# The gated-delta recurrence of a hybrid trunk layer: products of the inverse ahead of those of its transpose, in banks of their own, and another order around them

## The chip, the cores and the metric

The kernel runs on one core of a Trainium2 chip. The metric is the device time of one execution in microseconds. Three runs of the kernel before took 4781.29, 4789.78 and 4797.11 us; the median is 4789.78 us.

## The reference

One layer of a diffusion trunk is computed for 128 context tokens and 512 latent tokens, all in fp32: an adaLN-modulated RMSNorm, one input projection, two token mixers (a bidirectional chunked gated DeltaNet with 8 heads of 128, and a chunked spatial-gating MLP), branch and output projections, and a retrieval of experts (16384 single-neuron experts, 8 heads, top 16). What matters here is the DeltaNet:

```
S_t = exp(g_t) (I - beta_t k_t k_t^T) S_{t-1} + beta_t k_t v_t^T ;  o_t = S_t^T q_t / sqrt(dk)

decay = exp(where(causal, gc_i - gc_j, -inf))          # gc: cumulative log decay in a chunk
m   = where(strict, (beta k) k^T * decay, 0);  tri = m + I
u, w = tri^-1 [beta v, beta k exp(gc)]
qk  = q k^T * decay
per chunk:  v_new = u - w S
            o = (q exp(gc)) S + qk v_new
            S = S exp(g_last) + (k exp(g_last - gc))^T v_new
```

It runs forward and backward in time, for the context from a zero state, for the latent tokens from a given state.

## The kernel before, in words

The kernel takes chunks of 128 tokens, one a batch. The function `deltanet` runs once for the context (one block of tokens, two directions: two batches) and once for the latent tokens (four blocks, two directions: eight batches, n = 0 to 7). All eight heads of a batch are worked together. Five engines have instruction streams written out by hand, in a fixed order, tied by semaphores.

The inverse of `tri` is built by doubling. `x_` holds the inverse, `xt` its transpose, both 128 x 8 x 128, in two copies that alternate by batch. `begin` sets level 0 from the matrix m (`m_`) and its transpose (`mt`). For each level k = 1 to 6:

- POOL multiplies `mt` by the mask of the level (`masked`, L927) into one of two buffers `lev`;
- PE multiplies `lev` by `x_` (L992 or L999) into banks 4 and 5: the sub-products, in two halves u of four heads;
- ACT copies each half to `pm` (L1215);
- PE multiplies on the left by `xt` and on the right by `xt` (`changed_products`, L1010), giving what changes in `x_` (not at level 6) and in `xt`. Before, both results of a half lie side by side in bank 2 + u, and each half is released by one semaphore, `q_ps`;
- DVE adds them into `x_` and `xt`, four additions of 128x256 (L1142, L1144).

Around the levels, a batch also turns k and v by the identity (L987, into banks 6 and 7, and 0 and 1), multiplies them by gates on DVE (`kbe`, `kd`, `vn`), and prepares the next batch n + 1: PE makes the decay sums (`decays`, banks 0 and 1) and the gram matrix (banks 6 and 7) after level 4 and the q k scores (`scores_of`, banks 0 and 1) after level 5; DVE makes the `differences` for masking after level 4 (L1105, sixteen operations) and the `strict` product after level 5 (L1117, eight). In `finish` PE makes w (half_products into banks 4 and 5), turns m of the next batch (`turn_m`), and makes v_new (L1057, L1058), o (L1066, L1067) and the new state's addend. DVE then runs `begin` for the next batch (L1125 to L1134), takes o (L1178 or L1180, banks 4 and 5) and adds the state (L1185), which releases `batch_done`. PE's turning of k for the next batch waits for `batch_done`; so does POOL's `state` (L948: the state times its decay; then L951: queries times their decay). At the fifth latent batch (n = 4) the state is loaded anew for the other direction, after `batch_done`.

Beside this, 28 gathered rows of experts for the context tokens are used in the latent recurrence, four in each of the batches 0 to 6: POOL issues an indirect gather of 1 MB (`gather_until`, L350) into one of three slots, once the row that had the slot has been used, and DVE takes a dot product per row (`use_rows`, L396). Before, rows 0 to 3 of a batch are used ahead of level 1, after the additions of level 4, after the strict product of level 5, and between the two halves of o (in batch 0 the first at level 3). POOL issues the gathers after mask 3, after mask 6, and two after the first two masks of the next batch.

## Time and profile before

| | us |
|---|---|
| profiled execution, span from first to last instruction | 4786.7 |
| timed runs, median of 3 (4781.29 to 4797.11) | 4789.78 |
| latent recurrence, 1198.36 to 1569.04 of the span | 370.7 |
| steady latent batch (1248.03 to 1292.99) | 44.96 |

The span is that of one profiled execution; what lies around the span in that execution is not recorded separately, so the span stands beside the timed runs. In the rows below, times are microseconds from the start of the span. PE is TensorE, PEld its weight loads, DVE is VectorE, ACT is ScalarE, POOL is GpSimd. A timeline row gives the start, the duration, the engine, the line of the kernel, the operation, what it writes and reads, how many instructions are merged, and in brackets how long the engine was idle before it and whom it waited for.

### The profile page before, as it was taken

The numbers are of one execution on the slowest core, as the hardware profiler recorded it, in microseconds if no ns is written. First come the engines' busy times: TensorE is split into PE (matmuls) and PEld (weight loads), VectorE is DVE, ScalarE is ACT, GpSimd is POOL, SyncE is SP. The second block draws the span as 40 slices with busy tenths as digits, with TensorE's granted clock in tenths as the row PEclk, the third lists the DMA queues.
The fourth block names the chain that finished last, engine by engine and source line by source line (L and its number), as shares of the span: only waits on it lengthen the run. The fifth ranks groups of instructions, "written<-read, shape, count | busy, mean of one in ns | idle before, by whom it ended". The sixth has DMA issues, their size and how long they took to land.

```text
span 4786.7 us, 61495 instructions
## 1 busy us (share of the span) xinstructions
PE 4559.0 (95%) x25813; PEld 3365.2 (70%) x25813; DVE 3043.3 (64%) x4399; ACT 579.6 (12%) x1080; POOL 1656.3 (35%) x1110
## 2 busy tenths in 40 slices
PE   6989999999888999899999998999999999999997
PEld 2776346444888544347555545699999999999997
DVE  1451006888877777417777667988865557886556
ACT  1531001441222100000000001110000000000000
POOL 0131001674655554210544443433432332322221
PEclk8999999999999999999999999999999999999998
DMA  9919898997322998997999997579999999999998
GB/s 400 383 63 368 314 347 321 384 393 288 110 83 90 361 390 352 421 369 270 408 420 420 411 413 300 220 294 420 418 417 421 405 406 419 417 417 419 404 420 326
DMA packets 237328, 1663.47 MB, mean 348 GB/s; under 512 B 28231, under 2 KB 32729, under 8 KB 37787
## 3 DMA queue, kind: packets, MB, share of 16 engines
q0 software_dynamic: 130048, 939.72, 48.6%
q1 hardware_dynamic: 98884, 673.84, 35.6%
q10 hardware_dynamic: 8120, 45.98, 2.4%
q8 instruction: 204, 3.34, 0.3%
q14 instruction: 72, 0.58, 0.0%
HBM read 1639.68 MB, written 18.94 MB: 347 GB/s over the span
## 4 chain that ended last, share of the span: by engine, by line
PE 43%; DVE 6%; DMA 5%; issue 1%; POOL 1%; ACT 0%; ACTq 0%; DVEq 0%; POOLq 0%
PE ps L242 25%; PE ps L2415 14%; DMA arena_sb<-peer_v,arena_sb 4%; DVE arena_sb L401 2%; PE ps L2357 1%; PE ps L1815 1%; DMA arena_sb<-peer_u,arena_sb 1%; POOL arena_sb L350 1%; DMA x_rows<-arena_sb 0%; DVE arena_sb L2117 0%; DVE arena_sb L2107 0%; DVE arena_sb L2109 0%; DVE arena_sb L2190 0%; DMA arena_sb<-w_query 0%; DVE arena_sb L2114 0%
## 5 line engine op out<-in xcount | busy, mean ns | idle before, releaser
L242 PE MATMUL ps<-arena_sb 128*128 128x224 f32 (+3 forms) x9728 | 2292.2, 396 | 10.7 <-PEq L579 6.2
L242 PEld LDWEIGHTS ps<-arena_sb 128*128 128x128 f32 x9728 | 1669.6, 191 | 627.2 <-issue 335.0
L401 DVE SCALAR_TENSOR_TENSOR arena_sb<-arena_sb 128x2048 f32<-128x2048 f32 x412 | 988.7, 2400 | 460.8 <-DMA arena_sb<-peer_v,arena_sb 431.3
L396 DVE CUSTOM_DVE_ANT_0 arena_sb<-arena_sb 128x2048 f32<-128x2048 f32 x416 | 977.7, 2366 | 306.5 <-DMA arena_sb<-peer_u,arena_sb 305.8
L350 POOL DMA_INDIRECT arena_sb<-peer_v,arena_sb x416 | 617.6, 1485 | 1147.9 <-DVE arena_sb L401 918.4
L350 POOL DMA_INDIRECT arena_sb<-peer_u,arena_sb x416 | 642.2, 1544 | 811.2 <-DVE arena_sb L396 462.4
L2415 PE MATMUL ps<-arena_sb 128*128 128x224 f32 x4096 | 776.3, 352 | 1.3 <-ACT arena_sb L2454 0.6
L2415 PEld LDWEIGHTS ps<-arena_sb 128*128 128x128 f32 x4096 | 774.4, 190 | 1.9 <-issue 1.0
L1625 PE MATMUL ps<-arena_sb 128*128 128x512 f32 x768 | 342.8, 603 | 25.3 <-DMA arena_sb<-w_gb_r 10.2
L1625 PEld LDWEIGHTS ps<-arena_sb 128*128 128x128 f32 x768 | 145.6, 193 | 217.7 <-issue 197.0
L1815 PE MATMUL ps<-arena_sb 128*128 128x512 f32 x640 | 277.7, 596 | 4.4 <-DMA arena_sb<-w_out 2.2
L288 POOL DMA_DIRECT2D arena_sb<-w_mod x64 | 34.8, 544 | 590.8 <-PE ps L249 478.0
L1815 PEld LDWEIGHTS ps<-arena_sb 128*128 128x128 f32 x640 | 121.8, 191 | 159.5 <-issue 153.6
L927 POOL TENSOR_TENSOR arena_sb<-arena_sb 128x1024 f32<-128x1024 f32 x60 | 159.8, 2682 | 185.6 <-ACT arena_sb L1206 175.6
L1682 DVE TENSOR_TENSOR arena_sb<-ps,arena_sb 128x512 f32<-128x512 f32 x16 | 11.1, 692 | 288.9 <-PE ps L1625 288.9
L249 PE MATMUL ps<-arena_sb,scond_sb 128*32 128x512 f32 x768 | 128.4, 703 | 33.0 <-DMA arena_sb<-w_mod 33.0
L1340 PE MATMUL ps<-arena_sb 128*128 128x512 f32 x320 | 138.4, 593 | 0.8 <-DMA arena_sb<-w_vg 0.4
L1010 PE MATMUL ps<-arena_sb 128*64 128x32 f32 (+1 forms) x3520 | 122.9, 228 | 5.0 <-ACT arena_sb L1215 2.5
L1010 PEld LDWEIGHTS ps<-arena_sb 128*64 128x64 f32 x3520 | 114.0, 143 | 11.4 <-ACT arena_sb L1215 6.1
L2604 DVE TENSOR_SCALAR arena_sb<-arena_sb 128x128 f32<-128x128 f32 x448 | 119.7, 353 | 0.0
L1340 PEld LDWEIGHTS ps<-arena_sb 128*128 128x128 f32 x320 | 60.5, 190 | 78.1 <-issue 75.8
L2454 ACT ACTIVATE arena_sb<-ps 128x224 f32<-128x224 f32 (+27 forms) x107 | 28.9, 270 | 676.9 <-PE ps L242 676.9
(288 smaller groups left out, 2983.7 us busy)
## 6 DMA issues: line engine op xcount, KB each, us to landing
arena_sb<-peer_ut SPq DMA_DIRECT2D x128, 1024.0 KB, 9.3
arena_sb<-peer_vt SPq DMA_DIRECT2D x128, 1024.0 KB, 9.2
arena_sb<-w_mod POOLq DMA_DIRECT2D x64, 1024.0 KB, 9.2
arena_sb<-w_qkv SPq DMA_DIRECT2D x48, 1024.0 KB, 9.2
arena_sb<-w_out SPq DMA_DIRECT2D x48, 1024.0 KB, 7.4
arena_sb<-w_query SPq DMA_DIRECT2D x48, 1024.0 KB, 6.9
arena_sb<-w_mod SPq DMA_DIRECT2D x32, 1024.0 KB, 8.8
arena_sb<-w_ga_r SPq DMA_DIRECT2D x32, 1024.0 KB, 7.8
```

The costliest lines, as they stand in the source:

```text
L242: mm = pe.matmul(out, weights[:, k * P:(k + 1) * P], x[:, k, :], start=(k == 0), stop=(k == chunks - 1))
L249: mm = pe.matmul(out[32 * j:32 * j + 32, :], t.scond[:, k + j, :], weights[:, j * COL:(j + 1) * COL], start=start, stop=stop, tile_positio ...
L350: nc.gpsimd.indirect_dma_start(slot, None, a["peer_v" if adds else "peer_u"], bass.IndirectOffsetOnAxis(ap=seg.index[:, p:p + 1], axis=0)) ...
L396: nc.vector.tensor_tensor_reduce(rows, rows, total, 1.0, 0.0, ALU.mult, ALU.add, seg.dots[:, p:p + 1]).then_inc(t.rows_used, 1)
L401: nc.vector.scalar_tensor_tensor(out=total, in0=rows, scalar=seg.weight[:, p:p + 1], in1=total, op0=ALU.mult, op1=ALU.add).then_inc(t.rows ...
L927: nc.gpsimd.tensor_tensor(lev[:, k % 2], mt, over(nmask[:, 1 - r, k], H), ALU.mult).then_inc(s["level_masked"], 1)
L1010: mm = pe.matmul(compact(bank(2 + u), k, side)[rows, h % 4, a], lhs[:, h, rows], changed(rhs, k, second)[:, h, a], start=True, stop=True, ...
L1340: mm = pe.matmul(t.ps[:, 4 * c + b, :], h[:, k, b * P:(b + 1) * P], tile_slot(t, H + 4 * c + kq)[:, kk * COL:(kk + 1) * COL], start=(k == ...
L1625: mm = pe.matmul(t.ps[:, s, :], x[:, k, :], tile_slot(t, n)[:, kk * COL:(kk + 1) * COL], start=(k == 0), stop=(k == 4 * tiles - 1))
L1815: mm = pe.matmul(t.ps[:, 4 * (c % 2) + b, :], merged[:, k, b * P:(b + 1) * P], tile_slot(t, 4 * c + kq)[:, kk * COL:(kk + 1) * COL], start ...
L2415: mm = pe.matmul(t.ps[:, bank_of[h][first + i], 0:DENSE], ring[slot_of[n - 1]][:, col:col + P], acts[:, s, :], start=(s == 0 and h == 0), ...
L2604: nc.vector.tensor_scalar(weighted[i][:, u], t.pick_iota, key1[:, e:e + 1], weight[:, e:e + 1], ALU.is_equal, ALU.mult)
```

## The change

- The left products (what changes in `x_`) go to bank 2 for all eight heads, the right products (what changes in `xt`) to bank 3. All left products of a level are issued before the right ones, and each side has one semaphore (`left_ps`, `right_ps`) per level.
- DVE adds each side in one operation of 128x512 and releases `x_done` after the left one and `xt_done` after the right one. The sub-products of level k + 1 wait for `x_done` alone and are issued right behind the right products of level k.
- A batch starts with the sub-products of level 1; the turning of v and then of k follow them. Each half of those sub-products waits until DVE has read that half of the last o (`o_read`), since it overwrites its bank.
- For the next batch: decays are issued after the sub-products of level 4, the gram matrix after those of level 5, the scores after the last right products, ahead of w. `differences` is split: a half after level 4, a half after level 5; the strict product comes after level 6. ACT's exponents are split likewise.
- DVE makes `vn` at level 1, `kbe` at level 2 and `kd` at level 3.
- POOL makes mask 3 right behind the state's scaling, then two gathers, the staging of the next gates, masks 4 to 6, the queries' product, and a gather; after the first two masks of the next batch, one more.
- The 28 rows stay four a batch. Rows 0 to 3 are used ahead of level 1, at level 3, after `begin`, and between the halves of o. In batch 0, rows 0 and 1 are used after level 6, ahead of `begin`.

```diff
-            for u in range(2):
-                pe.wait_ge(s["x_done"], 13 * n + 1 + (2 * (k - 2) + u + 1 if k > 1 else 0))
-                products_of(4, u, lev[:, k % 2], x_[n % 2]).then_inc(s["p_ps"], 1)
-            for u in range(2):
-                pe.wait_ge(s["p_copied"], 12 * n + 2 * (k - 1) + u + 1)
-                if k < LEVELS - 1:
-                    changed_products(1, u, xt[n % 2], pm, k, r)
-                changed_products(0, u, pm, xt[n % 2], k, 1 - r).then_inc(s["q_ps"], 1)
+        def sub_products(n, k, u):
+            pe.wait_ge(s["level_masked"], 6 * n + k)
+            pe.wait_ge(s["x_done"], 6 * n + k)
+            if k == 1:
+                after(pe, s["o_read"], 2 * (n - 1) + u + 1)
+            products_of = paired_products if 1 < k < LEVELS - 1 else half_products
+            products_of(4, u, lev[:, k % 2], x_[n % 2]).then_inc(s["p_ps"], 1)
+        def left_products(n, r, k):
+            after(pe, s["xt_done"], 6 * n + k - 1)
+            for u in range(2):
+                pe.wait_ge(s["p_copied"], 12 * n + 2 * (k - 1) + u + 1)
+                mm = changed_products(2, u, xt[n % 2], pm, k, r)
+            mm.then_inc(s["left_ps"], 1)
+        def levels(n, r, j, b):
+            for u in range(2):
+                sub_products(n, 1, u)
+            pe.wait_ge(s["tok_done"], n + 1)
+            turned(0, tokens(heads[:, 16:24], b)).then_inc(s["vtok_ps"], 1)
+            after(pe, s["batch_done"], n)
+            pe.wait_ge(s["mt_copied"], 2 * n + 2)
+            turned(6, tokens(heads[:, 8:16], b)).then_inc(s["ktok_ps"], 1)
+            for k in range(1, LEVELS):
+                if k < LEVELS - 1:
+                    left_products(n, r, k)
+                right_products(n, r, k)
+                if k < LEVELS - 1:
+                    for u in range(2):
+                        sub_products(n, k + 1, u)
+                if n + 1 < 2 * nb:
+                    if k == 3:
+                        decays(n + 1, *order[n + 1])
+                    if k == 4:
+                        gram(n + 1, *order[n + 1])
         def finish(n, r, j, b):
+            if n + 1 < 2 * nb:
+                scores_of(n + 1, *order[n + 1])
...
@@ DVE
         def level(n, r, k):
+            if k < LEVELS - 1:
+                dve.wait_ge(s["left_ps"], 5 * n + k)
+                dve.wait_ge(s["x_done"], 6 * n + k)
+                cols = changed(x_[n % 2], k, r)
+                nc.vector.tensor_tensor(cols, cols, compact(2, k), ALU.add).then_inc(s["x_done"], 1)
+            dve.wait_ge(s["right_ps"], 6 * n + k)
+            after(dve, s["xt_done"], 6 * n + k - 1)
+            cols = changed(xt[n % 2], k, 1 - r)
+            nc.vector.tensor_tensor(cols, cols, compact(3, k), ALU.add).then_inc(s["xt_done"], 1)
...
+                elif k == 3:
+                    nc.vector.tensor_tensor(kd, banks(6), wide(tail, P), ALU.mult).then_inc(s["ktok_read"], 1)
+                    if n:
+                        use_rows(dve, nc, t, rows[1:2])
+                elif n + 1 < 2 * nb:
+                    if k == 6:
+                        strict(n + 1, *order[n + 1])
+                    else:
+                        differences(n + 1, k - 4, *order[n + 1])
+            if n == 0:
+                use_rows(dve, nc, t, rows[0:2])
             if n + 1 < 2 * nb:
                 begin(n + 1, *order[n + 1])
+            use_rows(dve, nc, t, rows[2:3])
...
@@ POOL
+            scale_state(n, *at)
+            masked(n, r, 3)
+            if 0 < n < loads:
+                gather_until(pool, nc, t, a, min(behind[n].start + 3, t.rows))
             if n + 1 < 2 * nb:
                 stage(n + 1, *order[n + 1])
+            for k in range(4, LEVELS):
+                masked(n, r, k)
+            scale_queries(n, *at)
+            if n == 0 and loads:
+                pool.wait_ge(h_out, 16)
+                gather_until(pool, nc, t, a, behind[0].start + 3)
+            elif n < loads:
+                gather_until(pool, nc, t, a, min(behind[n].start + 4, t.rows))
             if n + 1 < 2 * nb:
                 first_levels(n + 1, *order[n + 1])
             if n < loads:
+                gather_until(pool, nc, t, a, min(behind[n].start + 5, t.rows))
```

SP's loads of the next stage wait for `right_ps` at the point where they waited for `q_ps`. In the output projection the list of rows gets another length for groups whose entries are all zero.

## Rows read from the trace of the kernel before

**Rows 1.** The page, its part 1: busy time of the engines.

```profile
PE 4559.0 (95%) x25813; PEld 3365.2 (70%) x25813; DVE 3043.3 (64%) x4399; ACT 579.6 (12%) x1080; POOL 1656.3 (35%) x1110
```

**Rows 2.** Windows, one a latent batch: stretch, us, busy us, clock, DMA share, GB/s.

```profile
1198.36:1248.03 49.67, 42.32 (x672) 40.30 (x672) 41.73 (x67) 14.07 (x24) 29.29 (x16) 0.92 0.31 108
...
1248.03:1292.99 44.96, 39.53 (x680) 37.55 (x680) 38.59 (x67) 13.74 (x24) 28.73 (x14) 1.00 0.27 96
...
1337.95:1383.62 45.67, 41.33 (x680) 39.26 (x680) 38.39 (x67) 13.85 (x24) 28.77 (x14) 0.96 0.27 94
...
1383.62:1440.92 57.30, 45.27 (x680) 43.44 (x680) 38.38 (x67) 13.84 (x24) 27.03 (x14) 0.82 0.25 84
...
1532.30:1569.04 36.74, 35.39 (x620) 32.97 (x621) 14.36 (x29) 10.84 (x17) 13.69 (x6) 0.95 0.47 191
```

**Rows 3.** Timeline of PE in the steady batch (n = 1).

```profile
1248.09 1.09 PE L987 MATMUL ps<-ident_sb,arena_sb 128*128 128x128 f32 x8 [2.02 <-DVE arena_sb L1185]
...
1250.89 2.09 PE L1010 MATMUL ps<-arena_sb 128*64 128x64 f32 x64
...
1257.82 1.15 PE L999 MATMUL ps<-arena_sb 128*64 128x64 f32 x32 [1.40 <-POOL arena_sb L927]
...
1259.20 2.06 PE L1010 MATMUL ps<-arena_sb 128*64 128x32 f32 x64 [0.23 <-ACT arena_sb L1215]
...
1272.35 2.05 PE L982 MATMUL ps<-arena_sb 128*128 128x128 f32 x16 [0.42 <-DVE stat_sb L1109]
...
1276.12 1.44 PE L1010 MATMUL ps<-arena_sb 128*64 128x64 f32 x32
...
1278.29 2.05 PE L992 MATMUL ps<-arena_sb 128*128 128x128 f32 x16 [0.72 <-DVE arena_sb L1144]
```

**Rows 4.** Timeline of DVE at the end of that batch.

```profile
1273.55 2.15 DVE L1117 SCALAR_TENSOR_TENSOR arena_sb<-ps,beta_sb,arena_sb 128x128 f32<-128x128 f32 x8
...
1282.37 1.23 DVE L1132 TENSOR_TENSOR arena_sb<-arena_sb 128x1024 f32<-128x1024 f32 x1 [0.40 <-ACT arena_sb L1206]
...
1283.62 3.26 DVE L1134 TENSOR_TENSOR arena_sb<-arena_sb,ident_sb 128x1024 f32<-128x1024 f32 x1
...
1287.41 3.84 DVE L396 CUSTOM_DVE_ANT_0 arena_sb<-arena_sb 128x2048 f32<-128x2048 f32 x1
...
1291.17 0.68 DVE L1178 COPY arena_sb<-ps 128x512 f32<-128x512 f32 x1
...
1291.78 1.21 DVE L1185 TENSOR_TENSOR arena_sb<-arena_sb,ps 128x1024 f32<-128x1024 f32 x1
...
1292.90 2.28 DVE L396 CUSTOM_DVE_ANT_0 arena_sb<-arena_sb 128x2048 f32<-128x2048 f32 x1
```

**Rows 5.** Timeline of POOL over the same end and the next head.

```profile
1282.41 6.68 POOL L927 TENSOR_TENSOR arena_sb<-arena_sb 128x1024 f32<-128x1024 f32 x2 [13.07 <-ACT arena_sb L1206]
...
1289.25 2.85 POOL L350 DMA_INDIRECT arena_sb<-peer_u,arena_sb  x1 [0.15 <-issue]
...
1293.37 3.58 POOL L948 TENSOR_TENSOR arena_sb<-arena_sb 128x1024 f32<-128x1024 f32 x1
...
1297.04 2.39 POOL L951 TENSOR_TENSOR arena_sb<-arena_sb 128x1024 f32<-128x1024 f32 x1
...
1299.37 1.04 POOL L957 COPY gate_rows_sb<-g_sb 128x1024 f32<-128x1024 f32 x1
```

**Rows 6.** Timeline of POOL after the state's reload (n = 4).

```profile
1393.13 1.91 POOL L948 TENSOR_TENSOR arena_sb<-arena_sb 128x1024 f32<-128x1024 f32 x1 [9.15 <-issue]
```

**Rows 7.** Timeline of DVE at the head of the latent stage.

```profile
1191.57 3.37 DVE L1132 TENSOR_TENSOR arena_sb<-arena_sb 128x1024 f32<-128x1024 f32 x1
...
1194.97 3.24 DVE L1134 TENSOR_TENSOR arena_sb<-arena_sb,ident_sb 128x1024 f32<-128x1024 f32 x1
```

**Rows 8.** POOL's masks, L927: duration ns min/median/max, first and last start.

```profile
L927 POOL TENSOR_TENSOR arena_sb<-arena_sb x47: 2327/2367/3391, 1193.8 to 1547.9; 128x1024 f32<-128x1024 f32 x47
```

**Rows 9.** DMA issues of the latent stage: count and median us to landing.

```profile
arena_sb<-peer_u,arena_sb POOLq DMA_INDIRECT x28, 7.1
```

More of the change, by code:

```diff
@@ L960, in _ @@
         for n, at in enumerate(order):
[L961 removed]
+            r = at[0]
+            scale_state(n, *at)
+            masked(n, r, 3)
+            if 0 < n < loads:
+                gather_until(pool, nc, t, a, min(behind[n].start + 3, t.rows))
             if n + 1 < 2 * nb:
                 stage(n + 1, *order[n + 1])
[L964 to L970 removed]
+            for k in range(4, LEVELS):
[6 more added lines that the diff above has]
+                gather_until(pool, nc, t, a, min(behind[n].start + 4, t.rows))
             if n + 1 < 2 * nb:
@@ L973, in _ @@
             if n < loads:
-                gather_until(pool, nc, t, a, min(behind[n].start + 6, t.rows))
-            if n < loads:
-                gather_until(pool, nc, t, a, min(behind[n].start + 7, t.rows))
+                gather_until(pool, nc, t, a, min(behind[n].start + 5, t.rows))
     @block.tensor
@@ L1071, in _ @@
         decays(0, *order[0])
+        gram(0, *order[0])
         scores_of(0, *order[0])
@@ L1074, in _ @@
         for n, at in enumerate(order):
-            r, j, b = at
-            pe.wait_ge(s["tok_done"], n + 1)
-            turned(0, tokens(heads[:, 16:24], b)).then_inc(s["vtok_ps"], 1)
-            after(pe, s["batch_done"], n)
-            pe.wait_ge(s["mt_copied"], 2 * n + 2)
-            turned(6, tokens(heads[:, 8:16], b)).then_inc(s["ktok_ps"], 1)
-            for k in range(1, LEVELS):
-                level(n, r, k)
-                if n + 1 < 2 * nb:
-                    if k == 4:
-                        decays(n + 1, *order[n + 1])
-                    if k == 5:
-                        scores_of(n + 1, *order[n + 1])
+            levels(n, *at)
             finish(n, *at)
@@ L1177, in _ @@
                 if r == 0:
-                    nc.vector.tensor_copy(out, bank(4 + u))
+                    nc.vector.tensor_copy(out, bank(4 + u)).then_inc(s["o_read"], 1)
                 else:
-                    nc.vector.tensor_tensor(out, out, bank(4 + u), ALU.add)
-                if n < loads and u == 0:
-                    use_rows(dve, nc, t, behind[n][3:4])
+                    nc.vector.tensor_tensor(out, out, bank(4 + u), ALU.add).then_inc(s["o_read"], 1)
+                if u == 0:
+                    use_rows(dve, nc, t, rows[3:4])
             dve.wait_ge(s["state_scaled"], n + 1)
@@ L1208, in _ @@
         root(0)
-        exponents(0)
+        for u in range(2):
+            exponents(0, u)
         transposed(0)
```

119 lines of the change are left out of this document (51 added, 68 removed).

## The prediction

> **What bounds the kernel now.** I read the page first: TensorE is busy 95% [rows 1] of a span of 4786.7 us. An average over such different stages prices nothing, so I cut the recurrence with the view of windows, one window per batch, each ending where DVE's state addition (L1185) ends. Write B for that end. The reader is to see latent batches of 45 to 57 us, the last of 37, and a granted clock between 0.82 and 1.00 in them [rows 2]; from 1198.36 to 1569.04 they take 370.7 us, or 7.7% of the span. DMA's share is 0.25 to 0.47 there, so no stream of weights hides a change of this stretch. Last come the timelines of one steady batch: B = 1248.03 to B = 1292.99, 44.96 us at clock 1.00.
>
> In it PE is busy for 39.5 us and waits at four places: 2.02 us for B before it turns k; 1.40 us for the third mask from POOL; 0.42 us before the scores; 0.72 us before w [rows 3]. At the end it is DVE that sets B. Write M for the moment when the turned matrix has been copied (L1132 starts, 1282.37). From M to B are 10.62 us [rows 4], while PE has its last o and s products out 7.6 us after M.
>
> **Inside a level nothing is gained.** A level takes 1.38 us from the first sub-product to the first corrected product (1257.82 to 1259.20), then 2.06 us of products: 3.44 us [rows 3]. After: the left products (1.03) first, the right ones (1.03) behind them. The wide addition to x starts when the left ones have drained (some 0.17 us) and takes about 0.68, the nearest row being the 128x512 copy L1178 [rows 4]; 0.85 us of it fit behind 1.03 us of right products, so the next sub-products follow at once: 1.38 + 2.08 = 3.46. DVE has fewer instructions, which is worth nothing while PE sets the pace. Own banks and separate semaphores cost nothing either.
>
> **Steady batch after, from B to M.** PE's times after B:
> - Head. Sub-products 1 now come before the two turnings and half of them wait for `o_read` of the second half, about 1.15 us before B. So u1 runs to B - 0.2, v is turned to 0.8, k to 1.7, level 1 ends at 3.8. Before: k turned and sub-products (1248.09 to 1250.89), then level 1 (2.09), ended at 4.95 [rows 3]. Gain 1.2.
> - Levels 2 and 3 end at 7.24 and 10.7. The third mask is there: POOL's state scaling ends at 3.96 because it is pushed behind DVE's row (3.58 us instead of 1.91 [rows 5, 6]), the mask adds 2.35 [rows 8]: 6.3. The old stall of 1.40 is gone.
> - What is late next is the fourth mask. Behind the third stand two gathers (0.95 + 0.30 each, 2.5), the staging (1.04) and its own 2.35: 12.3. With row 0 not yet landed DVE loses the first place on the port and all is some 0.15 later. PE is ready at 10.7 to 11.8, so it stalls to 12.45.
> - Sub-products 4 (1.12), decays (1.88) and products (2.08): 17.53. The additions behind the row that now stands at level 3 come 0.2 late: 17.74. Level 5 with the gram matrix in its gap: 22.82. Both gaps hide 0.26 us of copying each. Sub-products 6 (1.88) and the last right products (1276.12 to 1277.56, 1.44 [rows 3]): 26.14, against 29.54 before.
> - Then scores (1.88, which cover DVE's last addition, so the 0.72 of before is saved), w (1.88), turning and copying m: M at 32.1, against 34.34. **Gain to M: 2.25 us.** The difference halves, 2.07 us each, follow the additions of levels 4 and 5 and end before the scores want them.
>
> **From M to B.** Here the change gives it back. Before, DVE after L1132 does L1134 (3.26), a half of o, a row (3.84, though the next one takes 2.28), a half of o, the state [rows 4]. After, the row that stood behind the strict products (L1117) stands here as well: 0.6 + 2.2 us more of DVE in front of a B that DVE sets. The rows show what it meets: DVE operations with both inputs in SBUF and POOL's masks do not overlap. POOL's two masks run 1282.41 to 1289.09 (6.68, where 2 x 2.35 would be 4.7), one of them and L1134 wait for each other, the row waits for the second, and the gather behind them takes 2.85 instead of 0.95 [rows 4, 5]. So after: masks gone at M + 6.7, row 2 to M + 8.8, o (0.60), row 3 (2.21), o (0.60), state (1.20): B = M + 13.4. And DVE is late: last addition, strict products (2.15 [rows 4]) and three passes of begin, some 1.14 each, end at M + 0.5, so that POOL takes the port first, as at the head of the stage where L1132 took 3.37 and L1134 3.24 [rows 7]. Then B = M + 14.0. Against 10.62: **loss 2.8 to 3.4 us**. Batch: 32.1 + 13.9 = 46.0, or **+1.05** (bounds -1.6, were none of it to wait for POOL: M + 11.3; and +2.4, were row 0 of the next batch late by as much as its gather can be: landing takes a median of 7.1 us from issue [rows 9], and its issue lies at the end of the masks, so that it lands about 1 us after B).
>
> The Trainium skill (SBUF — State Buffer, section Who interferes with whom) says that a DVE instruction with two SBUF inputs and a GpSimd one that reads SBUF exclude each other, and that issue order decides who blocks. The rows agree (3.26 against 1.23, 3.58 against 1.91); the rule speaks against moving a row behind `begin`, where both masks run.
>
> **The other batches.**
> - n = 0: PE turns v and k (1.9) after sub-products 1 instead of before; rows 0 and 1 (4.4) lie ahead of begin, and row 3 is gathered only after the next masks, and waits for its landing. The stall that row 1 made in this batch goes. By the same walk B comes 2.7 to 7.3 later than in its 49.67 us; I take +5.
> - n = 1, 2, 3, 5, 6: 5 x 1.05 = +5.2.
> - n = 4, state reloaded: POOL's scaling starts 9.5 us after B [rows 6], the third mask is now next (13.8 instead of 17.1 after B), but the fourth stands behind gathers and staging at 19.7. 55.5 against 57.30: -1.8 (bounds -4 and 0).
> - n = 7, no rows: head -1.2, w now waits for the whole last addition, +0.9: -0.3.
> - Context: masks of n = 1 start 2.39 earlier (the query product, L951 [rows 5], is now behind them), -0.6 in n = 0, +0.9 for the last w: -2.0.
> - Clock. The batch at 0.96 took 0.7 us more than the one at 1.00 [rows 2]. Now the head has two idle pieces of about 2 us with 0.94 of work between, where it had one of 2.02; I take three more batches at the lower level: +2.1 (bounds 0 and 12).
>
> The Trainium skill (TensorE: Matmul & The Clock Gate, section HAM oscillation) has it that waits between short bursts return the array to half clock again and again. This trace shows it in part: 0.82 in the batch with the long wait, 1.00 in one with four short ones [rows 2].
>
> Sum: 5 + 5.2 - 1.8 - 0.3 - 2.0 + 2.1 = +8.2 us on the profiled span of 4786.7. What lies around that span is not shown; the median of the timed runs, 4789.8, is 3.1 above it. Prediction **4798 us**. Row count after the stage, `behind` in the output projection and the loads of w_z are as before: 0, since the list only changes its length for groups whose entries are all zero.
>
> **Rivals.**
> - *Faster.* The tail: if POOL's masks let DVE through, row 2 ends 2.2 after L1134 and not after the masks, B = M + 11.3. Place: DVE between M and B; price -2.7 per row batch. It decides wherever the tail falls under 12.9 us after M, which is 10.62 + 2.25. Then six batches give -1.6, n = 0 about +1, n = 4 -4, context and n = 7 -2.3: about -15, or 4775. For: L1132 at 1.23 was let through before the mask. Against: L1134 (3.26) and the row behind it (3.84) [rows 4].
> - *Nothing gained or lost.* Only the order of DVE and POOL at M falls the lucky way and row 0 lands in time: +0.3 a batch, n = 0 +2.7, the rest -4: 4790.
> - *Slower by clock.* The two idle pieces bring the lower level in all batches, twice in some: 12 in place of 2: 4808.
> - *Slower by landing.* Row 0, gathered behind two masks, row 2 and its own 0.95, lands 2 to 3 us after B; left addition 1 stands behind it on DVE, and PE behind that. The fourth mask's stall absorbs 1.7 of it: +1.4 x 6: 4806.
> - That it doesn't do what it says: with no difference beyond the moved row, +2.2 x 7: 4805, held in the two above.
>
> **Numbers.** Forecast 0.42, faster rival 0.13, nothing 0.18, clock 0.15, landing 0.12. The range takes in the second, fourth and fifth and most of the first: 4780 to 4812. A time 0.3% (14.4 us) off 4789.8 can be told from no change: under 4775.4 faster, over 4804.2 slower. Half of the faster rival lies under its bound, and a little of my own error: 0.12. The two slow rivals and the upper end of the forecast: 0.27. Same: 0.61.
>
> **What would show it.** Steady batches of 46 us; third-mask stall gone, one of about 1.7 us before sub-products 4; no wait before w; M 2.2 us earlier after B; 13.4 to 14.0 us from M to B with two rows in it, the first stretched by POOL; PE idle before each half of sub-products 1; batch 0 longer than 50 us, batch 4 shorter than 57. Wrong if M to B stays under 13 us, or if level 5 waits for DVE.

## The result: 0.54% slower, and the profile after

The changed kernel takes 4816.52 us (median of 4 runs, 4811.15 to 4826.55) against 4788.06 us (4781.29 to 4797.11) for the kernel before: a ratio of 1.0054, 95% interval 1.0040 to 1.0069 (the ratio is an estimate of its own; the quotient of the two medians is 1.0059, inside the interval). Forecast were 4798 us; the measured time lies above the range.

Page, part 1, of the changed kernel: the engines do what they did [rows 1], in a longer span (4824.5 us; this profiled execution is the longest of the four).

```profile
PE 4571.3 (95%) x25813; PEld 3375.2 (70%) x25813; DVE 3053.1 (63%) x4289; ACT 576.1 (12%) x1080; POOL 1668.9 (35%) x1110
```

Windows of the changed kernel over the latent batches, each ending where the state addition (L1221 here, L1185 before) ends: stretch, us, busy us of PE, PEld, DVE, ACT and POOL, granted clock, DMA share, GB/s. The answers to [rows 2]:

```profile
1196.85:1248.70 51.85, 44.36 (x692) 42.68 (x693) 37.48 (x56) 14.22 (x25) 29.17 (x15) 0.89 0.28 103
...
1248.70:1297.32 48.62, 42.66 (x681) 40.83 (x681) 39.77 (x56) 13.51 (x24) 29.34 (x13) 0.92 0.25 88
...
1401.58:1455.85 54.27, 44.27 (x682) 42.33 (x681) 43.92 (x56) 13.51 (x24) 27.11 (x13) 0.88 0.26 88
...
1555.32:1592.32 37.00, 34.89 (x617) 32.79 (x617) 13.56 (x17) 9.81 (x16) 13.62 (x6) 0.94 0.46 191
```

The recurrence takes 395.47 us where it took 370.7. By batch, after minus before: +2.2 (n = 0), +3.7, +7.5, +6.2, -3.0 (n = 4), +3.7, +4.4, +0.3 (n = 7): +24.8. The medians differ by 28.5 and the spans of the two profiled executions by 37.8; of these another 14.5 stand behind the recurrence (3232.2 us for 3217.6) and -1.5 ahead of it. What stands behind it has no known cause: it varies from 3211.6 to 3236.0 among all the profiled executions here, and was 3218.0 in one of the changed order (e2). So the place was forecast rightly and the size was not. With B and M as in the prediction (M is where L1163, the old L1132, starts): M to B takes 13.42 in every steady batch, the predicted 13.4. What failed is B to M: 32.1 forecast; 35.2, 39.0, 38.4, 35.8 and 36.8 measured.

Timeline of PE in batch 1 of the changed kernel (B = 1248.70), the answer to [rows 3]: start, us, engine, line, operation, idle time before and its releaser.

```profile
1247.72 2.05 PE L996 MATMUL ps<-arena_sb 128*128 128x128 f32 x8 [1.19 <-DVE arena_sb L1214]
...
1249.56 3.46 PE L991 MATMUL ps<-ident_sb,arena_sb 128*128 128x128 f32 x16
...
1252.95 2.10 PE L1014 MATMUL ps<-arena_sb 128*64 128x64 f32 x64
1254.99 1.15 PE L1003 MATMUL ps<-arena_sb 128*64 128x64 f32 x32
...
1258.46 1.15 PE L1003 MATMUL ps<-arena_sb 128*64 128x64 f32 x32
...
1269.19 1.15 PE L1003 MATMUL ps<-arena_sb 128*64 128x64 f32 x32 [1.37 <-DVE arena_sb L1172]
...
1276.22 1.44 PE L1014 MATMUL ps<-arena_sb 128*64 128x64 f32 x32
```

The reader is to see two things. The head runs at half clock (granted clock 0.53 from 1247.72 to 1253.00): eight products in 2.05 us (1.06 at full clock), the sixteen turnings in 3.46 (eight take 1.09 at full clock [rows 3]), so that level 1 ends 6.3 us after B and not 3.8. And level 5 waits 1.37 us for the left addition. The levels between go at the predicted 3.46 (sub-products at 1254.99 and 1258.46 are 3.47 apart), the third mask's stall is gone, and so is the wait before the scores and before w.

Why the left addition is late: DVE, then POOL, then PE, in batch 2 (B = 1297.32).

```profile
1311.96 6.51 DVE L396 CUSTOM_DVE_ANT_0 arena_sb<-arena_sb 128x2048 f32<-128x2048 f32 x1
...
1318.40 0.68 DVE L1172 TENSOR_TENSOR arena_sb<-arena_sb,ps 128x512 f32<-128x512 f32 x1
```

```profile
1307.02 6.98 POOL L927 TENSOR_TENSOR arena_sb<-arena_sb 128x1024 f32<-128x1024 f32 x3
...
1313.98 2.34 POOL L952 TENSOR_TENSOR arena_sb<-arena_sb 128x1024 f32<-128x1024 f32 x1
```

```profile
1319.22 1.98 PE L1003 MATMUL ps<-arena_sb 128*64 128x64 f32 x32 [3.98 <-DVE arena_sb L1172]
...
1321.13 3.60 PE L986 MATMUL ps<-arena_sb 128*128 128x128 f32 x16
```

Row 1 (L396), now at level 3, is issued at 1311.96. POOL is then in the three masks that it has run back to back since 1307.02, with the query product next; it is through with all four at 1316.32. The row ends 2.15 us after that, at 1318.47, so it ran its own 2.28 [rows 4] from there. It did not take its turn after the mask that was running (the third, to 1314.00): it waited for the query product behind it as well. In batches 3 and 4 the row is issued during the second of the masks, waits for the rest of it, the third and the query product, and takes 7.11 and 7.92. The left addition follows at 1318.40, PE has waited 3.98 us, and the wait is followed by half clock (1.98 for 1.15, 3.60 for 2.05; granted clock 0.55 from 1319.20 to 1325.00).

In batch 1 mask 6 had itself waited for PE, and the row waited for that one operation alone. DVE, then POOL:

```profile
1264.67 3.77 DVE L396 CUSTOM_DVE_ANT_0 arena_sb<-arena_sb 128x2048 f32<-128x2048 f32 x1
```

```profile
1263.93 2.36 POOL L927 TENSOR_TENSOR arena_sb<-arena_sb 128x1024 f32<-128x1024 f32 x1 [0.85 <-PE ps L1003]
...
1266.24 4.41 POOL L952 TENSOR_TENSOR arena_sb<-arena_sb 128x1024 f32<-128x1024 f32 x1
```

POOL's query product is then the one that waits for the row (4.41 for 2.34). Batches 5 and 6 are the same (POOL had paused 0.52 and 0.89 before mask 6; the rows took 3.89 and 3.77). So the row waits through operations that POOL runs without a pause, and gets in behind the running one where POOL had paused just before it. That the former had already been issued when the row came is our reading; the trace shows the order, not why a pause changes it. The tail of that batch, DVE, the answer to [rows 4]:

```profile
1283.91 3.38 DVE L1163 TENSOR_TENSOR arena_sb<-arena_sb 128x1024 f32<-128x1024 f32 x1
...
1287.32 3.25 DVE L1165 TENSOR_TENSOR arena_sb<-arena_sb,ident_sb 128x1024 f32<-128x1024 f32 x1
...
1290.50 2.28 DVE L396 CUSTOM_DVE_ANT_0 arena_sb<-arena_sb 128x2048 f32<-128x2048 f32 x1
...
1293.31 2.27 DVE L396 CUSTOM_DVE_ANT_0 arena_sb<-arena_sb 128x2048 f32<-128x2048 f32 x1
...
1296.12 1.20 DVE L1221 TENSOR_TENSOR arena_sb<-arena_sb,ps 128x1024 f32<-128x1024 f32 x1
```

Here the masks end at 1289.50, L1165 gets through behind them, and both rows take their bare 2.28: the sum of 13.42 that was forecast.

A stretch whose two ends don't move with the rows is that from the end of the last addition (level 6) to B. DVE's last addition in batch 1 of the changed kernel, then in the kernel before:

```profile
1277.71 0.69 DVE L1176 TENSOR_TENSOR arena_sb<-arena_sb,ps 128x512 f32<-128x512 f32 x1 [0.52 <-PE ps L1014]
```

```profile
1277.83 0.74 DVE L1144 TENSOR_TENSOR arena_sb<-arena_sb,ps 128x256 f32<-128x256 f32 x2
```

To B these are 18.9 and 14.4 us, the same in each of the batches 1 to 6. The changed kernel has 4.5 us more of DVE there, in every one: the strict products (2.15) and row 2 (2.28) have moved into it.

### The profile page after: what moved, and what is told of

It reads as the page before. It is cut to its first block, busy times and chain, and to the rows that moved or that the text cites. A ratio compares the mean times of both kernels' runs of the same rounds, so it can differ in the third digit from the quotient of the medians.

```text
span 4824.5 us, 61547 instructions
## 1 busy us (share of the span) xinstructions
PE 4571.3 (95%) x25813; PEld 3375.2 (70%) x25813; DVE 3053.1 (63%) x4289; ACT 576.1 (12%) x1080; POOL 1668.9 (35%) x1110
## 4 chain that ended last, share of the span: by engine, by line
PE 30%; DMA 14%; DVE 8%; issue 2%; POOL 1%; ACT 0%; ACTq 0%; DVEq 0%; POOLq 0%
PE ps L242 20%; DMA arena_sb<-peer_v,arena_sb 11%; PE ps L2452 8%; DVE arena_sb L401 3%; DMA arena_sb<-peer_u,arena_sb 2%; POOL arena_sb L350 1%; PE ps L1852 1%; PE ps L2394 1%; DMA x_rows<-arena_sb 0%; DVE arena_sb L2641 0%; DVE arena_sb L2154 0%; DVE arena_sb L2144 0%; DVE arena_sb L2146 0%; DVE arena_sb L2227 0%; DMA arena_sb<-w_query 0%
## 5 line engine op out<-in xcount | busy, mean ns | idle before, releaser
L396 DVE CUSTOM_DVE_ANT_0 arena_sb<-arena_sb 128x2048 f32<-128x2048 f32 x416 | 982.0, 2376 | 299.6 <-DMA arena_sb<-peer_u,arena_sb 299.1
L350 POOL DMA_INDIRECT arena_sb<-peer_v,arena_sb x416 | 627.6, 1509 | 1148.1 <-DVE arena_sb L401 958.2
L927 POOL TENSOR_TENSOR arena_sb<-arena_sb 128x1024 f32<-128x1024 f32 x60 | 156.1, 2616 | 188.9 <-ACT arena_sb L1242 169.5
L996 PE MATMUL ps<-arena_sb 128*128 128x128 f32 x640 | 94.9, 304 | 46.1 <-DVE arena_sb L1214 18.0
```

The lines of the kernel that those rows point to most:

```text
L350: nc.gpsimd.indirect_dma_start(slot, None, a["peer_v" if adds else "peer_u"], bass.IndirectOffsetOnAxis(ap=seg.index[:, p:p + 1], axis=0)) ...
L396: nc.vector.tensor_tensor_reduce(rows, rows, total, 1.0, 0.0, ALU.mult, ALU.add, seg.dots[:, p:p + 1]).then_inc(t.rows_used, 1)
L927: nc.gpsimd.tensor_tensor(lev[:, k % 2], mt, over(nmask[:, 1 - r, k], H), ALU.mult).then_inc(s["level_masked"], 1)
L996: mm = pe.matmul(bank(out + u)[:, h % 4], lhs[:, h], rhs[:, h], start=True, stop=True)
```

## Experiments

Each is a version of the changed kernel (two are of the kernel before). "Recurrence" is from the first sub-products to the last B of the profiled execution; "row 1" is what the six rows 1 of the batches 1 to 6 took together, 13.7 if nothing disturbs them. All ratios are to the kernel before, with 95% intervals. The ratios come from the timed runs, the two other columns from one profiled execution each, and these were not all typical: that of the changed kernel was the slowest of its 4 (10.0 us over the median), that of e9 the slowest of its 12 (13.5 over), those of e4 and e12 the fastest (9.1 and 9.0 under), that of e2 14.0 under. A few us between two recurrences show nothing by themselves.

| version | ratio | recurrence us | row 1 us |
|---|---|---|---|
| kernel before | 1 | 370.7 | 14.4 |
| after | 1.0054 (1.0040 to 1.0069) | 395.5 | 33.0 |
| e1 rows 1 and 2 back | 1.0008 (0.9996 to 1.0020) | 373.2 | 14.0 |
| e2 row 1 back | 1.0026 (1.0013 to 1.0039) | 377.2 | 14.9 |
| e3 row 2 back | 1.0054 (1.0036 to 1.0071) | 384.7 | 31.8 |
| e4 before, rows moved | 1.0031 (1.0019 to 1.0043) | 385.4 | 25.8 |
| e5 after, short dots | 0.9949 (0.9924 to 0.9975) | 347.9 | |
| e6 before, short dots | 0.9943 (0.9924 to 0.9961) | 346.7 | |
| e7 query product waits | 1.0046 (1.0033 to 1.0060) | 395.9 | 23.4 |
| e8 v turned first | 1.0023 (1.0009 to 1.0036) | 384.5 | 23.4 |
| e9 is e1 with e8 | 0.9990 (0.9980 to 1.0000) | 370.4 | 14.7 |
| e10 is e9, gathers apart | 0.9987 (0.9976 to 0.9999) | 370.8 | 25.5 |
| e11 is e5 with e8 | 0.9950 (0.9931 to 0.9969) | 345.7 | |
| e12 is e10, query product late | 0.9975 (0.9964 to 0.9987) | 355.1 | 13.7 |

**e1, e2, e3: the rows' places.** Row 1 goes back to level 4, row 2 back ahead of `begin`; together and one by one.

```diff
@@ row 1
-                    if n:
-                        use_rows(dve, nc, t, rows[1:2])
...
                     else:
+                        if n and k == 4:
+                            use_rows(dve, nc, t, rows[1:2])
                         differences(n + 1, k - 4, *order[n + 1])
@@ row 2
             if n == 0:
                 use_rows(dve, nc, t, rows[0:2])
+            else:
+                use_rows(dve, nc, t, rows[2:3])
             if n + 1 < 2 * nb:
                 begin(n + 1, *order[n + 1])
-            use_rows(dve, nc, t, rows[2:3])
+            if n == 0:
+                use_rows(dve, nc, t, rows[2:3])
```

> The changed kernel, but in batches 1 to 6 row 1 is used after the additions of level 4 (not at level 3) and row 2 after the strict product (not after begin); PE's and POOL's order as changed. Theory A (the rows' places cost the time: row 1 waits for the masks and the query product that POOL has already issued, and holds left addition 4; row 2 lengthens DVE's tail): M to B falls from 13.4 to about 10.7 us, the stall before sub-products 5 falls from 1.4 to 4.0 us to under 1.5, the latent batches take 43 to 46 us and the whole 15 to 30 us less than the changed kernel: about level with the kernel before. Rival (PE's new order itself costs, by idle pieces in the head and the lower clock): under 8 us less.

> The changed kernel with row 1 alone put back behind the additions of level 4. Theory A: the 3.8 to 7.9 us of row 1 become 2.3 to 3.5, B to M falls by 1 to 5 us a batch, M to B stays 13.4: 6 to 14 us less in all. Rival (the row's 2.2 us are due somewhere anyway, and at level 4 they hold left addition 5 as long): under 4 us less.

> The changed kernel with row 2 alone put back ahead of begin. Theory A: M to B falls by 2 to 2.8 us, B to M stays (35 to 41 us): 8 to 16 us less in all. Rival (DVE's work from the last level to B is one sum, whatever its order): under 4 us less.

With both back the loss is gone to within the interval: 373.2 us. This is a sum of two parts: batch 4 is 8.7 us shorter than in the kernel before (more on it below), the other batches together 11.2 longer. Row 1 alone brings 18 of the 22 us of the recurrence, by the ratios 13 of 22 us. DVE in batch 2 of e1, at level 4, and POOL's last operation ahead of it:

```profile
1318.13 2.34 DVE L396 CUSTOM_DVE_ANT_0 arena_sb<-arena_sb 128x2048 f32<-128x2048 f32 x1
```

```profile
1315.63 2.38 POOL L952 TENSOR_TENSOR arena_sb<-arena_sb 128x1024 f32<-128x1024 f32 x1
```

POOL's chain ends at 1318.01, the row starts at 1318.13 and meets nothing. Row 2 alone brings nothing in the timed ratio (a miss: a gain of 8 to 16 us was expected), though M to B falls from 13.42 to 9.17: M itself moves, since the row now stands ahead of it. DVE's tail in e3, batch 2:

```profile
1339.56 3.37 DVE L1163 TENSOR_TENSOR arena_sb<-arena_sb 128x1024 f32<-128x1024 f32 x1
...
1342.96 1.23 DVE L1165 TENSOR_TENSOR arena_sb<-arena_sb,ident_sb 128x1024 f32<-128x1024 f32 x1
...
1344.71 2.28 DVE L396 CUSTOM_DVE_ANT_0 arena_sb<-arena_sb 128x2048 f32<-128x2048 f32 x1
```

From the last level to B, DVE's work is nearly one sum: from the last addition to B it is 18.93 in the changed kernel, e2, e7 and e8, and 17.80 in e1, e3, e9, e10 and e12, the same in all six batches. So the place of row 2 in it is worth 1.13 us a batch (behind the row L1165 takes 1.23 and not 3.25, while the pass two operations earlier takes 2.25 and not 1.21), and not the 4.25 by which M to B falls. Six batches make 6.8 us: e1 is 8.6 us under e2 by the medians of one session, and between e3 and the changed kernel so little is not resolved (their intervals are 0.3% wide). M to B alone was the wrong stretch to read: the row that left it went to another place of the same sum.

**e4: the moves alone.** In the kernel before, row 1 is put at level 3 and row 2 behind `begin`, as the change has them; nothing else.

> The kernel before, but in batches 1 to 6 row 1 is used at the end of level 3 and row 2 after begin; all else as before. Theory A (the places of the rows are the loss): M to B grows from 10.6 to about 13.2 us, row 1 takes over 3 us behind POOL's masks; 12 to 30 us slower than the kernel before. Rival (only together with PE's new order do they cost): under 8 us slower.

385.4 us, 15 more than before, 1.0031 (the changed kernel: 25 and 1.0054). DVE in batch 1:

```profile
1258.25 4.99 DVE L396 CUSTOM_DVE_ANT_0 arena_sb<-arena_sb 128x2048 f32<-128x2048 f32 x1
```

So more than half of the loss does not need the new order of the products; the rest comes only with it.

**e5, e6: no rows to speak of.** The dot products take 64 of the 2048 elements (the rest of each product is left out), in the kernel after and in the one before.

```diff
+        if t.short_dots:
+            rows, total = rows[:, 0:64], total[:, 0:64]
         nc.vector.tensor_tensor_reduce(rows, rows, total, 1.0, 0.0, ALU.mult, ALU.add,
...
```

> The changed kernel with the 28 dot products in the latent recurrence taken over 64 of their 2048 elements (the rest of each product is left out); gathers, waits and order stay. Its partner is the kernel before with the same cut. Theory A (the rows are what the new order collides with): M to B falls from 13.4 to about 9 us, the stall of left addition 4 goes, B to M is 32.6 us at the full clock, a batch 41 to 42 us, and it is 0 to 12 us faster than its partner. Rival (the new order of PE, with its split head, loses by itself): over 5 us slower than its partner.

> The kernel before with the same cut of the 28 dot products. Both theories: row 2's 0.72 us and the 3.84 us of row 3 go, a batch falls from 44.96 to 41.5 to 43 us, 15 to 28 us faster than the kernel before in all.

Without rows the two kernels are alike (347.9 and 346.7), but not batch by batch: batch 4 is 4.9 us shorter after (47.4 for 52.3), the five steady ones are 0.5 to 1.9 longer, 42.3 to 43.7 us for 41.8 to 42.3. So the new order shows none of the 2.25 us a batch that the prediction counted in front of M. The comparison is not quite fair to it: with short dots POOL's scaling is no longer held up by row 0, and the 1.40 stall for the third mask, a part of those 2.25, is gone from the kernel before too. And in the steady batches the last addition does end 0.2 to 1.7 us earlier after B than in e6; but from there to B e5 takes 14.80 and e6 12.65, 2.15 more, as much as the strict products [rows 4] that now stand there. DVE at the start of batch 2 of e5 (B = 1293.59), then PE:

```profile
1296.63 1.37 DVE L399 CUSTOM_DVE_ANT_0 arena_sb<-arena_sb 128x64 f32<-128x64 f32 x1 [3.04 <-DMA arena_sb<-peer_u,arena_sb]
```

```profile
1298.75 1.15 PE L1006 MATMUL ps<-arena_sb 128*64 128x64 f32 x32 [1.08 <-DVE arena_sb L1176]
```

Row 0, gathered behind both masks, lands 3.0 us after B; DVE waits for it with the left addition behind it, and PE loses 1.08. That is the predicted rival of the landing, seen only in the two versions of the changed kernel with short dots (e5, e11): with full rows row 0 starts at B in every version.

**e7: what the row waits for.** POOL's query product waits until level 4's addition is done, so that it isn't issued when row 1 starts.

```diff
+            if 0 < n < loads:
+                pool.wait_ge(s["xt_done"], 6 * n + 4)
             scale_queries(n, *at)
```

> The changed kernel in which POOL's query product waits, in batches 1 to 6, until the transposed additions of level 4 are done. Theory A1 (row 1 on DVE waits for every POOL operation issued ahead of it): one operation fewer stands ahead, row 1 falls from 6.5 to 7.9 us in batches 2 to 4 to about 4.2 to 5.6, 3.8 us in the others stay; 4 to 9 us less in all. Rival A2 (DVE and POOL take turns, one operation each, and the 6.5 us come from the masks alone): no change of row 1, under 2 us in all.

DVE in batch 2, and POOL around it:

```profile
1316.91 3.90 DVE L396 CUSTOM_DVE_ANT_0 arena_sb<-arena_sb 128x2048 f32<-128x2048 f32 x1
```

```profile
1316.31 2.35 POOL L927 TENSOR_TENSOR arena_sb<-arena_sb 128x1024 f32<-128x1024 f32 x1 [1.01 <-PE ps L1005]
...
1322.09 2.37 POOL L952 TENSOR_TENSOR arena_sb<-arena_sb 128x1024 f32<-128x1024 f32 x1 [3.43 <-DVE arena_sb L1178]
```

The row waits for the one mask that is running, to 1318.66, and takes its 2.28: 3.8 to 4.2 us in all six batches, none of 6.5 to 7.9. Nothing is gained (395.9 us; 4 to 9 us less were expected). And as a test of the rule it is weaker than it looks: in five of the six batches POOL had paused before mask 6, and after such a pause the changed kernel too has rows of 3.8 to 3.9. Batch 4 alone has the masks without a pause, and there the row takes 4.18 where it took 7.92. The better test of the query product is e12 against e10, below. PE reached level 3 late in these batches. In the profile of e7 its corrected products waited up to 2.2 us for ACT's copies some 10 us after B, and row 1 was issued only 16.7 to 18.8 after B, where it was 14.0 to 16.0.

**e8, e9: the head.** v's half of the turnings goes ahead of sub-products 1; e9 has the rows back as well.

```diff
-            for u in range(2):
-                sub_products(n, 1, u)
             pe.wait_ge(s["tok_done"], n + 1)
             turned(0, tokens(heads[:, 16:24], b)).then_inc(s["vtok_ps"], 1)
+            for u in range(2):
+                sub_products(n, 1, u)
```

> The changed kernel with v turned ahead of the first sub-products, where PE idles for DVE's reading of o. Theory B (the head's two idle pieces cost the clock, and 0.9 us of turning stands behind B for nothing): level 1 ends 0.9 us earlier after B, more where the lower clock goes; clock of the batches over 0.93 instead of 0.88 to 0.92; 6 to 15 us less. Rival (the fourth mask and row 1 absorb the head, so that it hides): under 4 us less.

> Both corrections in the changed kernel: row 1 behind the additions of level 4 and row 2 ahead of begin (batches 1 to 6), and v turned ahead of the first sub-products. Alone the rows gave back all but 4 us, and v 13 us of the 26. Theory (the two add, the rows' places and the head's clock): 4 to 14 us faster than the kernel before, batches of 44 to 46 us at a clock over 0.95. Rival (they hide each other: with the shorter tail the head has no long idle pieces to fill): within 3 us of the run with the rows alone, 2 to 6 us slower than the kernel before.

e8 fell where the clock theory had it, but it doesn't show that theory: its rows 1 took 23.4 us and not 33.0, so up to 9.6 of the 11 us of the recurrence can be the row's: in its batches 2 and 6 the row met no POOL operation at all, since mask 6 had waited for PE. The clean comparison is e9 with e1, both with undisturbed rows: 370.4 against 373.2, and by the ratios 0.9990 against 1.0008, 0.18% or 8.6 us, with intervals that just overlap. So the head's order is worth something like 3 to 9 us. Where it comes from can be read: at full clock level 1 ends 3.2 after B with v first and 3.9 without; e9 has 3.2 in five of six batches, e1 has 3.9 to 6.9. In e8, with the longer tail, it is 3.2 in three and 5.3 to 5.9 in the others. PE in e10 (head of batch 2), where the head meets the full clock:

```profile
1295.21 1.13 PE L998 MATMUL ps<-arena_sb 128*128 128x128 f32 x8 [1.68 <-DVE arena_sb L1219]
...
1296.24 1.09 PE L993 MATMUL ps<-ident_sb,arena_sb 128*128 128x128 f32 x8
```

and the same eight products and eight turnings in the head of e8's batch 1, at half clock (batch 1 has it in e9, e10 and e12 too; it follows a wait of over 4 us at the end of batch 0):

```profile
1243.19 2.05 PE L996 MATMUL ps<-arena_sb 128*128 128x128 f32 x8 [1.14 <-DVE arena_sb L1214]
...
1245.03 1.92 PE L991 MATMUL ps<-ident_sb,arena_sb 128*128 128x128 f32 x8
```

**e10, e12: POOL's chain out of the row's way.** e10 issues the second gather behind mask 4; e12 also holds the query product back until level 5's addition.

```diff
@@ e10
-                gather_until(pool, nc, t, a, min(behind[n].start + 3, t.rows))
+                gather_until(pool, nc, t, a, min(behind[n].start + 2, t.rows))
...
             for k in range(4, LEVELS):
                 masked(n, r, k)
+                if 0 < n < loads and k == 4:
+                    gather_until(pool, nc, t, a, min(behind[n].start + 3, t.rows))
@@ e12
+            if 0 < n < loads:
+                pool.wait_ge(s["xt_done"], 6 * n + 5)
             scale_queries(n, *at)
```

> As the one with both corrections, and of POOL's two gathers behind mask 3 the second stands behind mask 4. Mask 4 comes 1.25 us earlier. Theory (mask 4 is what PE waits for at level 4, 0.8 to 1.8 us a batch): 4 to 8 us less than the one with both corrections. Rival (the gather is late for row 2, or PE's wait returns at mask 5 or at DVE): no gain.

> The previous best version (rows 1 and 2 back, v turned ahead of sub-products 1, second gather behind mask 4) with one more edit: POOL's query product waits for level 5's addition in batches 1 to 6. In the previous version row 1 starts 16.6 us after B in batches 2 to 6 and takes 4.5 us, since the query product has already been issued, and PE then waits 2.9 us before the halves at the gap of level 5. Theory A (the row waits for every POOL operation already issued): with only the two masks ahead, which end just as the row starts, the row takes 2.3 to 2.5 us, PE's wait falls to about 0.7, a batch gets 1.5 to 2.2 us shorter in five batches: recurrence 360 to 363 us where it was 370.8, median 0.15 to 0.25% below the previous version, ratio to before 0.9962 to 0.9974. Rival D (the end of a batch is the sum of DVE's work behind the last level and of the gathers' landing, and the query product only moves its collision to another operation of DVE): row 1 shorter, but the batches stay within 0.5 us of 47, recurrence 369 to 372, ratio 0.998 to 0.9995.

e10 is not to be told from e9 (4 to 8 us less were expected). Its trace has the reason: levels arrive earlier and the row meets the query product again, 4.5 us in five batches of six: it starts as mask 6 ends and waits for the whole of the product behind it. PE in its batch 2, ahead of the halves at level 5:

```profile
1320.13 2.90 PE L998 MATMUL ps<-arena_sb 128*128 128x128 f32 x16 [2.90 <-DVE arena_sb L1174]
```

With the query product held back, POOL, DVE and PE in the same batch of e12 (B = 1291.87):

```profile
1303.85 4.68 POOL L927 TENSOR_TENSOR arena_sb<-arena_sb 128x1024 f32<-128x1024 f32 x2
...
1314.12 2.37 POOL L952 TENSOR_TENSOR arena_sb<-arena_sb 128x1024 f32<-128x1024 f32 x1 [5.60 <-DVE arena_sb L1180]
```

```profile
1308.49 2.28 DVE L396 CUSTOM_DVE_ANT_0 arena_sb<-arena_sb 128x2048 f32<-128x2048 f32 x1
```

```profile
1313.59 2.02 PE L1000 MATMUL ps<-arena_sb 128*128 128x128 f32 x16 [0.69 <-DVE arena_sb L1176]
```

The masks end at 1308.53 as the row starts; it takes 2.28, PE waits 0.69 and the query product (2.37) runs where it neither delays nor is delayed. Windows of e12, batches 1 and 2:

```profile
1244.81:1291.87 47.06, 42.02 (x685) 40.07 (x684) 37.19 (x56) 13.63 (x24) 27.23 (x13) 0.95 0.26 91
...
1291.87:1335.52 43.65, 39.57 (x679) 37.76 (x678) 37.18 (x56) 13.62 (x24) 27.20 (x13) 0.99 0.29 98
```

Batches of 43.7 to 45.7 us (but for 47.1 in the first), a recurrence of 355.1, and 4779.33 us against 4792.27: 0.9975 (0.9964 to 0.9987), the fastest of the versions that leave nothing out. Against e10, from which it differs in the one wait, the six batches are 13.5 us shorter in the two profiles, but 0.12%, some 6 us, by the ratios, whose intervals overlap; 0.15 to 0.25% were expected. Theory A asked for 360 to 363 and a ratio of 0.9962 to 0.9974: the trace lies under the first, the timed runs at the edge of the second. What is plain is the row (2.28 for 4.5) and PE's wait behind it (0.69 for 2.90); the clock is at 0.96 to 1.00 in the batches 2 to 6, and no wait of PE there is over 1.7 us.

**Batch 4, in all versions.** Of the 15.6 us that e12's recurrence is under that of the kernel before, 11.7 stand in batch 4, the one with the reload of the state (45.65 for 57.30); the five steady batches give 3.0. SP's load of the state, 512 KB, issued at B of that batch, in the kernel before and in the changed one; the last number is the time to landing in us.

```profile
arena_sb<-state SPq DMA_DIRECT2D x1, 512.0 KB, 9.4
```

```profile
arena_sb<-state SPq DMA_DIRECT2D x1, 512.0 KB, 4.1
```

POOL's scaling of the state follows at 9.5 after B before [rows 6], and in the changed kernel (B = 1401.58) at 4.2:

```profile
1405.78 1.92 POOL L947 TENSOR_TENSOR arena_sb<-arena_sb 128x1024 f32<-128x1024 f32 x1 [10.11 <-issue]
```

The landing goes with POOL's gathers of 1 MB ahead of it. Where two were issued 0.6 to 3.7 us before B (the kernel before, e6) the load took 9.1 and 9.4; where the last one was issued 6.7 to 7.7 before (the changed kernel, e1 to e3, e7 to e10, e12) it took 3.9 to 4.4; in between (e4, e5, e11) 4.9 to 5.7. The new order of POOL moves the gathers away from it. No version was made for this alone, so that the gathers are the cause is argued from these fourteen profiles and not shown by an edit of its own.

**e11: the head without rows.**

> The changed kernel with the 28 dot products over 64 of 2048 elements (the rest left out) and v turned first. The same cut in the kernel before gave 4764, in the changed kernel 4772 (0.6% and 0.5% under the kernel before). Theory (what the new order of PE still loses there is row 0 landing about 3 us after B, ahead of which left addition 1 can't go): row 0 is waited for as long, and v first moves nothing: 4766 to 4774. Rival (the order loses by the turnings behind B): 5 to 9 us less, level with or under the cut kernel before.

0.9950, as e5: with rows out of the way the landing of row 0 holds the batch, and the head's order brings 2 us in the trace and nothing that is measured.

## Why the prediction was wrong

- *The sum*: +8.2 forecast. Measured in the recurrence are +2.2 for the +5 of batch 0, +25.4 for the +5.2 of the five steady batches, -3.0 for -1.8 in batch 4, +0.3 for -0.3 in n = 7. The steady batches are the miss.
- *The failed step* is in the steady batch: "The additions behind the row that now stands at level 3 come 0.2 late: 17.74." The row was taken to be undisturbed but for the end of one mask. It took 3.8 to 7.9 us, PE waited 1.4 to 4.7 for the addition in five of six batches, and half clock followed in the worst batches (in the sixth, n = 5, PE stood 2.20 us amid the decays, with nothing in the profile that it waited for, and met the row's end without a wait). The prediction had the exclusion of the two engines, and priced it in the tail; it did not lay row 1's new place beside POOL's own queue, whose start it had worked out one item earlier (fourth mask at 12.3; by its own prices two more and the query product without a break last to about 19). e1, e2 and e4 show this term; e12 against e10 shows what the query product has in it, and batch 4 of e7.
- *A second step failed ahead of it*: level 1 was to end 3.8 after B and ended at 5.3 to 6.8, since the head ran at half clock. At full clock it is 3.9 (batches 4 and 5 of e1), so the sum was right and the clock was not. Sub-products 4 hide most of it: they were to wait for their mask until 12.45 and started at 12.2 to 14.0. M was late by 3.1 to 6.9, so most of that arose behind them, where row 1 stands.
- *The clock* was sized at +2.1 for three batches. The batches 1 to 6 have 0.88 to 0.92 where five of them had 0.96 to 1.00 and one 0.82. The rival "slower by clock" (4808) named the two idle pieces of the head as the cause. They did bring half clock in the head of all of the batches 1 to 6, so this rival had a true part. e9 has one of them filled and gives 3 to 9 us over e1; with the row's wait gone too (e12) the clock is 0.96 and more in five of six batches. Both waits lower it; how much of the loss is the wait itself and how much the clock behind it was not measured apart.
- *The gain ahead of M*, 2.25 a batch, did not come even without rows (e5 against e6). There the head was not to blame: it ran at full clock in five of six batches, with level 1 done at 4.1. The landing of row 0 held level 2, the strict products stand ahead of M, and e6 has lost the stall for the third mask as well.
- *M to B* was sized rightly (13.42; 13.4 to 14.0 forecast), but it is no stretch of its own: in e3 it is 9.17, and the stretch from the last addition to B is only 1.13 shorter. The whole tail was forecast well: from the last right products to B 19.9 for 15.4 before, 4.4 more, and 4.5 more were measured from the last addition.
- *Held*: the third mask's stall gone; levels of 3.46; no wait before w; batch 0 over 50 (51.85; 54.7 forecast) and batch 4 under 57 (54.27; 55.5 forecast). Batch 4 is luck: its fourth mask was forecast at 19.7 after B, with the scaling at 9.5, and ended at 14.2, since the state landed 5.3 us earlier; against that row 1 took 7.92 there and PE waited 4.65. The stall of 1.7 before sub-products 4 came only in batch 4 (0.68): PE was late itself. n = 7: +0.3 for -0.3. Context: +0.1 for -2.0; its own batch 0 was not charged with the turnings behind sub-products 1, as the latent one was.
- *Rivals*: "faster" ruled out (its sum counts six steady batches beside n = 4, where there are five); "nothing" is the time that the change has with rows 1 and 2 back (e1), though not for the rival's reason, but because batch 4 gives what the others lose; "landing" is real where the dots are short (e5, e11), and did not occur with full rows.

The Trainium skill (SBUF — State Buffer, section Who interferes with whom) says that a DVE instruction with two SBUF inputs contends with a GpSimd instruction that reads SBUF, and that issue order decides who blocks. The traces agree for a single operation (3.77 in batch 1 of the changed kernel) and show more where GpSimd's operations stand in a row: DVE stayed blocked through the rest of a mask and the query product (6.51), and through one mask more (7.11, 7.92).

## What to carry to other kernels

A DVE operation with both inputs in SBUF is to be placed against POOL's queue, not against POOL's busy share: list what POOL runs there without a pause, and charge all of it. Where the row must stay, hold POOL's next movable operation back with a wait on work that DVE finishes after the row (e12: one wait, 2.2 us a row in five batches; by the timed runs some 6 us, within their noise). When an operation moves along one engine, read the stretch between two points that are fixed from outside (here from the last addition to B), not to a marker that moves with it. And read a sum of batches batch by batch: here one that gains hides others that lose.

## What was not expected of the hardware

- DVE's row waits for all of POOL's operations that run without a pause: 6.5 to 7.9 us for 2.28, and 3.8 where POOL had to wait for PE just before the running one.
- Half clock after short waits. In the head of the changed kernel PE waits, makes eight products, waits again and makes eight more, the last in 2.04 to 2.05 us in all of the batches 1 to 6 (1.06 to 1.13 at full clock). Batch 3:

```profile
1345.95 1.13 PE L996 MATMUL ps<-arena_sb 128*128 128x128 f32 x8 [2.31 <-DVE arena_sb L1214]
1348.76 2.05 PE L996 MATMUL ps<-arena_sb 128*128 128x128 f32 x8 [1.68 <-DVE arena_sb L1214]
```

  With waits of 0.31 and 1.68 at the same place (e10, batch 2) the last eight took 1.13, and with one wait of 2.02 the kernel before kept its full clock [rows 3].
- A load of 512 KB took 9.1 to 9.4 us with two gathers of 1 MB issued just ahead of it, and 3.9 to 4.4 with none so near.
- ACT's copies of the sub-products start about 1.5 us late in some batches, some 10 us after B, and PE waits 2.2 for them. PE in batch 2 of e9:

```profile
1303.46 2.09 PE L1014 MATMUL ps<-arena_sb 128*64 128x32 f32 x64 [2.21 <-ACT arena_sb L1255]
```

The two gathers are issued next to each other just then; in e10, where they are apart, the wait is 0.86. That the gathers cause it was not tested and stays open, as does what lies outside the recurrence: 3.7 us of the medians' difference, 13.0 us of the spans' difference.
